# Moving the diagonal matrix of a gather step behind the dot product of the following step

## The chip, the cores and the metric

The kernel runs on one core of a Trainium2 chip. The time is that of one execution on the device, in microseconds (us). The core has a matmul engine (TensorE, PE in the profile; its weight loads are PEld), a vector engine (VectorE, DVE), an activation engine (ScalarE, ACT), a general engine (GpSimd, POOL) that here issues the gathers, and SyncE (SP), which issues the plain transfers. Each engine executes its own instructions in the order written and waits for the others by semaphores.

## The reference

One inference step of an encoder of two layers for 256 prompt tokens and 32 sample tokens, 1024 features each. Each layer is a mixer (a gated delta rule with a linear recurrence in layer 0, differential attention in layer 1) and behind it a channel mixer with 16,384 experts of a single neuron. The expert part is what this change touches:

```python
qry = (xb @ w_query).reshape(PEER_BLOCK, PEER_HEADS, 2, PEER_DQ // 2)
sc = jnp.einsum('thpd,pnd->thpn', qry, sub_keys)
s1, i1 = lax.top_k(sc[:, :, 0], PEER_TOPK)
s2, i2 = lax.top_k(sc[:, :, 1], PEER_TOPK)
...
top_s, sel = lax.top_k(cand_s, PEER_TOPK)
idx = jnp.take_along_axis(cand_i, sel, axis=-1)
gate = jax.nn.softmax(top_s, axis=-1)
act = jax.nn.gelu(jnp.einsum('thed,td->the', u_emb[idx], xb))
return jnp.einsum('the,thed->td', gate * act, v_emb[idx])
```

Each token has 8 heads of 16 chosen experts, 128 in all. For each chosen expert a row u and a row v of 1024 floats are gathered; the dot product of u with the token goes through a gelu, is multiplied by the gate, and weights v in the sum.

## The kernel before

Work on the experts is cut into 576 **gather steps**, numbered m from 0. A step handles 128 tokens with one expert each: a gather of 128 rows of 8 KB (u and v side by side, 1 MB) into one of the 8 slots of the ring `UV`, slot m % 8. Four engines take part, each in the order of m:

- POOL waits until the slot is free (`uv_free`) and issues the gather (L510). A list of 8 indices is copied ahead (L503).
- DVE waits for the landing, computes the 128 dot products (L1131), waits for the gelu of the same step, and builds the diagonal matrix DG = identity × gelu × gate (L1134). At each step with c = m % 16 = 0 it first copies the 16 gates of the next 16 steps (L1126), and at c = 15 it waits for its last diagonal.
- ACT applies the gelu to the dot products (L706).
- PE waits for the diagonal and multiplies it with the v half of the slot, as four matmul records into the accumulator in PSUM (L1510), and then frees the slot. The sum over the 128 experts of a token is thus formed in PSUM.

The steps form six units, which begin at m = 0, 32, 160, 288, 320 and 448: per layer 32 steps of sample tokens and twice 128 of prompt tokens. All units begin at c = 0 and end at c = 15. At the end of a unit PE closes the accumulator (L1523), and DVE adds it to the residual (L1149); PE begins the next unit only behind that.

Other work is put between the steps, by hand, at written step numbers: each engine calls `upto` to do its steps up to some m and then does its part of a mixer. `loop` does 16 steps an iteration. The order is: the first 32 steps between picks; a loop of 8 iterations over the steps 32 to 159, in which each iteration begins with a pick (the top-16 search of one head: L1072 to L1102) for later steps; then steps 160 to 447, with the mixer of layer 1 between them; and a last loop over the steps 448 to 575, with nothing between. The numbers for the middle part come from a table made by `step_plan`:

```python
for ps, m, misc, qkv, head, smp, out, q in ((0, 160) + PACE[0], (1, AHEAD) + PACE[1]):
    for kind, n, k in (("norm2", 1, misc), ("qkv", 24, qkv), ("head", 10, head), ("smp", 4 * (1 - ps), smp),
                       ("on", 1, misc), ("out", 8, out), ("norm3", 1, misc), ("q", 18 - 2 * ps, q)):
```

PE uses the same table but lags two steps behind it (PE_LAG = 2), except next to the edge of a unit: when PE reaches the mixer work of number m, it has done the steps up to m − 3.

Two **pick stages** matter below. In each, PE computes 16 query blocks (L1315) and their scores (L1553, L1555, or L1558), one pair of blocks for each pick of DVE; ScalarE copies blocks (L731) and scores (L723 to L726) out of PSUM in program order with its gelus. The first stage lies at the numbers 248, 251, 253, 256 and so on to 291, the second at 398, 400 and so on to 428. PE does a block, then the scores of the block before it. DVE does its steps up to the number of the odd block of a pair, then the pick of the pair before.

Of the kernel before, what the change touches and what calls it, by code (L numbers as in the profile page):

```python
# [29 lines left out]
UVS = 8  # L30
# [42 lines left out]
def build(nc, T):  # L73
# [4 lines left out]
    ALU, ACT, AX = mybir.AluOpType, mybir.ActivationFunctionType, mybir.AxisListType  # L78

    with ExitStack() as ctx:  # L80
        def sb(name, shape, dt=F):
            return ctx.enter_context(nc.sbuf_tensor("sb_" + name, shape, dt))
# [3 lines left out]
        def S(name):  # L86
            if name not in sems:
                sems[name] = ctx.enter_context(nc.semaphore(name))
            return sems[name]
# [41 lines left out]
        ident = sb("ident", [128, 128])  # L131
# [118 lines left out]
        gl = sb("gl", [128, 8])  # L250
        gst = sb("gst", [128, 16])
        DG = sb("DG", [128, UVS, 128])
# [32 lines left out]
        def at(i, value):  # L285

            return value if i is None else i * 16 + value

        class Steps:
# [6 lines left out]
            def edge(self, which):  # L296
                for q, (_, _, first, n) in enumerate(UNITS):
                    if which == "begin" and self.m == first:
                        self.begin(q)
                    if which == "end" and self.m == first + n:  # L300
                        self.end(q)
# [534 lines left out]
        def _(eng):  # L836
            v = nc.vector
# [111 lines left out]
            for bt, (u0, u1) in enumerate(BT):  # L949
# [14 lines left out]
                for u in range(u0, u1):  # L964
                    c = c0 + 128 * (u - u0)
# [139 lines left out]
            def gate_of(q):  # L1105
# [10 lines left out]
                ch.link(v.reciprocal(gsum[:, 0:nh], gsum[:, 0:nh]))  # L1116
                ch.link(v.tensor_tensor(gt, gt, top.to_broadcast([128, nh, 16]), ALU.mult))

            def step(m, i=None):

                q = max(k for k in range(6) if UNITS[k][2] <= m)
                c0, xt, m0, _ = UNITS[q]
                c, sl = m % 16, m % UVS
                if c == 0:
                    g0 = c0 + m - m0
                    v.tensor_copy(gst[:, :], gate[:, g0:g0 + 16] if i is None else gate[:, bass.ds(i * 16 + g0, 16)])\  # L1126
                        .then_inc(S("gates"), 1)
                    eng.wait_ge(S("gates"), m // 16 + 1 if i is None else i + (m // 16 + 1))
                landed = 16 * (m // UVS + 1)
                eng.wait_ge(S(f"uv_in{sl}"), landed if i is None else i * 32 + landed)  # L1130
                v.tensor_tensor_reduce(UV[:, sl, 0:D], UV[:, sl, 0:D], Hn[:, xt, :], 1.0, 0.0,  # L1131
                                       ALU.mult, ALU.add, dots[:, sl:sl + 1]).then_inc(S("dots"), 1)
                eng.wait_ge(S("gelu"), at(i, m + 1))
                v.tensor_scalar(DG[:, sl, :], ident[:, :], gl[:, sl:sl + 1], gst[:, c:c + 1],  # L1134
                                ALU.mult, ALU.mult).then_inc(S("diag"), 1)
                if c == 15:
                    eng.wait_ge(S("diag"), at(i, m + 1))

            def end(q):
# [7 lines left out]
                for half in range(2):  # L1147
                    o = X[:, xt, 512 * half:512 * half + 512]
                    r = v.tensor_tensor(o, o, PS[:, 6 + half, :], ALU.add)  # L1149
                    if half:  # L1150
                        r.then_inc(S("x_peer"), 1)

            run = Steps(eng, step, end=end)

            def picks(ps, upto):
# [603 lines left out]
```

## Time and profile before

| what | value |
| --- | --- |
| time, median of 3 runs | 2196.11 us |
| the runs | 2196.11, 2195.97, 2197.49 us |
| span of the profiled execution | 2197.3 us |
| mean granted clock of TensorE | 0.915 |
| busy: PE, DVE, POOL, ACT | 1761.6, 1405.6, 691.1, 379.4 us |
| moved from and to memory | 696.16 MB, 317 GB/s on average |
| gathered by POOL's queue | 604.02 MB, 68.9% of the 16 DMA engines' span |

The page gives busy time and idle time by groups of instructions. A row such as "x2304 | 1144.1, 641 | 301.1 <-DVE" reads: 2304 instructions, busy 1144.1 us in all, 641 ns each, and 301.1 us in which their engine was idle just before one of them, mostly until DVE released it. A timeline row has the start in us from the begin of the span, the duration, engine, line, operation, output and input, how many neighbouring instructions are merged (x), and in brackets the idle time ahead of it and what ended that. A row of PE with x4 is one gather step, x8 two, x12 three. A window's row has the stretch and its length, then the busy time (and count) of PE, PEld, DVE, ACT and POOL, TensorE's granted clock (1.00 is full speed), the DMA share and GB/s. A row of the chain of waits is start, duration, and the piece of work.

### The profile page before, as it was taken

What the parts mean: (1) busy time and instruction counts of PE and PEld (TensorE: products, weight loads), DVE (VectorE), ACT (ScalarE), POOL (GpSimd) and SP (SyncE); (2) the same over time, 40 slices, a digit from 0 to 9 for tenths busy, and PEclk for the clock granted to TensorE, in tenths of its full rate; (3) what the DMA queues carried; (4) which work ended last, traced back from release to release, by engine and by line L of the source; (5) the groups of instructions that cost most, each with busy time, mean ns of one, the idle gap of its engine ahead of it and who ended that gap; (6) DMA issues with size and microseconds to landing.
All of it is one profiled execution on the core that took longest, in us unless ns stands there. A gap on an engine that the chain in (4) does not pass through costs nothing.

```text
span 2197.3 us, 21194 instructions
## 1 busy us (share of the span) xinstructions
PE 1761.6 (80%) x6456; PEld 1001.9 (46%) x6456; DVE 1405.6 (64%) x3449; ACT 379.4 (17%) x1208; POOL 691.1 (31%) x738
## 2 busy tenths in 40 slices
PE   7978888777767778988698875998878877777776
PEld 6767875323223325754265542554445543322222
DVE  4464258877777774356446887554665896766665
ACT  2242022100000002142202111101421101111111
POOL 2032101334434451233223221333333324444441
PEclk9989999898878889999799987999889988999999
DMA  4310226889998999999688975999989978999997
GB/s 148 116 75 1 68 87 249 324 330 388 388 388 354 383 383 376 372 327 359 264 319 339 390 299 197 398 418 421 363 318 419 408 293 331 390 422 422 422 422 303
DMA packets 108846, 696.16 MB, mean 317 GB/s; under 512 B 12640, under 2 KB 12768, under 8 KB 34528
## 3 DMA queue, kind: packets, MB, share of 16 engines
q0 software_dynamic: 82944, 604.02, 68.9%
q1 hardware_dynamic: 24960, 89.98, 10.9%
q10 hardware_dynamic: 864, 1.16, 0.1%
q8 instruction: 44, 0.72, 0.1%
q14 instruction: 34, 0.28, 0.0%
HBM read 690.20 MB, written 4.90 MB: 316 GB/s over the span
## 4 chain that ended last, share of the span: by engine, by line
PE 45%; DVE 23%; DMA 19%; issue 7%; ACT 3%; POOL 1%; DVEq 0%; POOLq 0%; SPq 0%; ACTq 0%
PE PS L1510 21%; DMA sb_AR<-in_uv,sb_idst 19%; PE PS L1315 11%; DVE sb_AR L1131 5%; PE PS L1493 4%; DVE sb_DG L1134 2%; PE PS L1428 2%; PE PS L1591 2%; DVE sb_AR L1082 1%; DVE sb_AR L1075 1%; POOL sb_AR L510 1%; ACT sb_gl L706 1%; DVE sb_AR L1076 1%; DVE sb_AR L1079 1%; DVE sb_AR L1072 1%
## 5 line engine op out<-in xcount | busy, mean ns | idle before, releaser
L1510 PE MATMUL PS<-sb_AR,sb_DG 128*128 128x512 f32 x2304 | 1144.1, 641 | 301.1 <-DVE sb_DG L1134 285.3
L510 POOL DMA_INDIRECT sb_AR<-in_uv,sb_idst x576 | 610.8, 1060 | 1176.5 <-PE PS L1510 1118.0
L1510 PEld LDWEIGHTS PS<-sb_AR,sb_DG 128*128 128x128 f32 x2304 | 443.5, 204 | 916.7 <-DVE sb_DG L1134 463.2
L1131 DVE CUSTOM_DVE_ANT_0 sb_AR<-sb_AR,sb_Hn 128x1024 f32<-128x1024 f32 x576 | 704.6, 1223 | 160.3 <-DMA sb_AR<-in_uv,sb_idst 156.6
L1134 DVE TENSOR_SCALAR sb_DG<-sb_ident,sb_gl,sb_gst 128x128 f32<-128x128 f32 x576 | 222.7, 387 | 273.7 <-ACT sb_gl L706 273.7
L706 ACT ACTIVATE sb_gl<-sb_dots 128x1 f32<-128x1 f32 x576 | 116.7, 203 | 1228.3 <-DVE sb_dots L1131 1227.8
L1315 PE MATMUL PS<-sb_hT,sb_W 128*128 128x288 f32 (+2 forms) x1664 | 297.7, 335 | 0.8 <-ACT sb_hT L568 0.8
L1315 PEld LDWEIGHTS PS<-sb_hT,sb_W 128*128 128x128 f32 x1664 | 257.2, 192 | 64.3 <-issue 30.3
L1493 PEld LDWEIGHTS PS<-sb_W,sb_mixT 128*128 128x128 f32 x768 | 90.7, 196 | 9.8 <-issue 7.7
L1493 PE MATMUL PS<-sb_W,sb_mixT 128*128 128x128 f32 x768 | 90.9, 279 | 1.7 <-DVE sb_mixT L1045 1.7
L503 POOL COPY sb_idst<-sb_idx 128x8 uint32 (+1 forms) x72 | 24.4, 339 | 118.7 <-DVE sb_idx L1102 118.3
L1059 DVE TENSOR_TENSOR sb_X<-sb_X,PS 128x512 f32<-128x512 f32 x12 | 7.7, 684 | 77.4 <-PE PS L1493 77.4
L1072 DVE MAX8 sb_AR<-sb_AR 128x8 f32<-128x128 f32 (+1 forms) x108 | 32.8, 332 | 26.0 <-ACT sb_AR L726 20.1
L1591 PEld LDWEIGHTS PS<-sb_W,sb_hT 128*128 128x128 f32 x384 | 45.4, 192 | 7.7 <-issue 7.7
L1131 DVE DVE_READ_ACCUMULATOR2_ANT sb_dots<- 128x1 f32 x576 | 48.1, 83 | 0.0
L706 ACT ACT_TABLE_LOAD x36 | 46.2, 1283 | 3.0 <-DVE sb_dots L1131 1.8
L1302 PE MATMUL PS<-sb_ident,sb_Hn 128*128 128x128 f32 x96 | 20.7, 386 | 32.3 <-DVE sb_Hn L857 32.3
L1591 PE MATMUL PS<-sb_W,sb_hT 128*128 128x128 f32 x384 | 45.5, 275 | 0.0
L1079 DVE MAX8 sb_AR<-sb_AR 128x8 f32<-128x128 f32 (+1 forms) x108 | 32.9, 333 | 4.1
L1075 DVE FIND_INDEX8 sb_AR<-sb_AR 128x8 uint32<-128x128 f32 (+1 forms) x108 | 35.6, 329 | 0.0
L1082 DVE FIND_INDEX8 sb_AR<-sb_AR 128x8 uint32<-128x128 f32 (+1 forms) x108 | 34.7, 329 | 0.0
L1076 DVE MATCH_REPLACE8 sb_AR<-sb_AR 128x128 f32<-128x128 f32 (+1 forms) x108 | 34.6, 320 | 0.0
(315 smaller groups left out, 1101.6 us busy)
## 6 DMA issues: line engine op xcount, KB each, us to landing
sb_W<-in_w SPq DMA_DIRECT2D x144, 512.0 KB, 7.2
sb_AR<-in_uv,sb_idst POOLq DMA_INDIRECT x576, 11.3
sb_gB<-in_gains SPq DMA_DIRECT2D x7, 512.0 KB, 8.0
sb_AR<-in_kc SPq DMA_DIRECT2D x2, 1024.0 KB, 9.7
sb_AR<-in_vc SPq DMA_DIRECT2D x2, 1024.0 KB, 17.9
sb_X<-in_x SPq DMA_DIRECT2D x3, 512.0 KB, 5.2
out_o_v<-sb_AR SPq DMA_DIRECT2D x1, 1536.0 KB, 17.4
out_o_y<-sb_Hn SPq DMA_DIRECT2D x3, 512.0 KB, 7.4
```

The lines of the kernel that those rows point to most:

```text
L510: g.indirect_dma_start(UV[:, s, :], None, T[f"uv{l}"], bass.IndirectOffsetOnAxis(ap=idst[:, 8 * half + s:8 * half + s + 1], axis=0)).then_ ...
L706: s.activation(gl[:, o:o + 1], dots[:, o:o + 1], ACT.Gelu_apprx_tanh).then_inc(S("gelu"), 1)
L1075: ch.add(v.max_index(ind(i)[:, 0:8], val(i)[:, 0:8], src(i)))
L1076: ch.add(v.match_replace(tmp(i), val(i)[:, 0:8], src(i), -3.0e38))
L1079: ch.add(v.max(val(i)[:, 8:16], tmp(i)))
L1082: ch.add(v.max_index(ind(i)[:, 8:16], val(i)[:, 8:16], tmp(i)))
L1131: v.tensor_tensor_reduce(UV[:, sl, 0:D], UV[:, sl, 0:D], Hn[:, xt, :], 1.0, 0.0, ALU.mult, ALU.add, dots[:, sl:sl + 1]).then_inc(S("dots"), 1)
L1134: v.tensor_scalar(DG[:, sl, :], ident[:, :], gl[:, sl:sl + 1], gst[:, c:c + 1], ALU.mult, ALU.mult).then_inc(S("diag"), 1)
L1315: r = mm(PS[:, bank, 0:n], blkw(bb % WSLOTS, k), hT[:, k, c0:c0 + n], start=(k == 0), stop=(k == KT - 1))
L1493: r = mm(PS[:, 2 * t + j // 4, 128 * (j % 4):128 * (j % 4) + 128], mixT[:, k, 128 * t:128 * t + 128], blkw(bb % WSLOTS, k), start=(k == 0) ...
L1510: r = mm(PS[:, 6 + half, :], DG[:, sl, :], UV[:, sl, o:o + 512], start=False, stop=False, skip_group_check=True)
L1591: r = mm(PS[:, j % 4, 128 * i:128 * i + 128], hT[:, k, c:c + 128], blkw(bb % WSLOTS, k), start=(k == 0), stop=(k == KT - 1))
```

## The change

DVE's gather step no longer waits for its own gelu. The diagonal of step m − 1 is built behind the dot product of step m. Only at c = 15, the last of 16 steps, are two diagonals built, that of m − 1 and that of m, so that nothing is left over at the end of 16 steps. A step with c = 0 builds none. Whatever DVE does between two calls of `upto`, it does with the last diagonal still to come, unless the last step had c = 15. The other engines' programs are as they were.

```diff
+            def diagonal(m, i):
+
+                c, sl = m % 16, m % UVS
+                eng.wait_ge(S("gelu"), at(i, m + 1))
+                v.tensor_scalar(DG[:, sl, :], ident[:, :], gl[:, sl:sl + 1], gst[:, c:c + 1],
+                                ALU.mult, ALU.mult).then_inc(S("diag"), 1)
+
             def step(m, i=None):
...
                 v.tensor_tensor_reduce(UV[:, sl, 0:D], UV[:, sl, 0:D], Hn[:, xt, :], 1.0, 0.0,
                                        ALU.mult, ALU.add, dots[:, sl:sl + 1]).then_inc(S("dots"), 1)
-                eng.wait_ge(S("gelu"), at(i, m + 1))
-                v.tensor_scalar(DG[:, sl, :], ident[:, :], gl[:, sl:sl + 1], gst[:, c:c + 1],
-                                ALU.mult, ALU.mult).then_inc(S("diag"), 1)
+                if c:
+                    diagonal(m - 1, i)
                 if c == 15:
+                    diagonal(m, i)
                     eng.wait_ge(S("diag"), at(i, m + 1))
```

## Rows read from the trace of the kernel before

**Rows 1.** Page: chain by engine, two groups (busy, mean | idle before, releaser).

```profile
PE 45%; DVE 23%; DMA 19%; issue 7%; ACT 3%; POOL 1%; DVEq 0%; POOLq 0%; SPq 0%; ACTq 0%
...
L1510 PE MATMUL PS<-sb_AR,sb_DG 128*128 128x512 f32 x2304 | 1144.1, 641 | 301.1 <-DVE sb_DG L1134 285.3
...
L1134 DVE TENSOR_SCALAR sb_DG<-sb_ident,sb_gl,sb_gst 128x128 f32<-128x128 f32 x576 | 222.7, 387 | 273.7 <-ACT sb_gl L706 273.7
```

**Rows 2.** Windows: stretch, length, busy by engine, granted clock, DMA share, GB/s.

```profile
520.00:565.00 45.00, 30.86 (x64) 12.76 (x64) 34.26 (x87) 3.25 (x16) 16.23 (x18) 0.84 0.94 383
...
845.00:950.00 105.00, 104.53 (x609) 81.56 (x608) 36.24 (x75) 13.98 (x65) 23.17 (x27) 1.00 0.93 356
...
1210.00:1260.00 50.00, 43.98 (x178) 26.85 (x178) 44.79 (x140) 7.06 (x31) 14.36 (x16) 0.97 0.99 387
...
1700.00:1760.00 60.00, 52.09 (x233) 32.50 (x231) 52.28 (x171) 6.43 (x31) 18.89 (x21) 0.94 1.01 408
...
2000.00:2120.00 120.00, 95.58 (x193) 32.81 (x194) 76.90 (x148) 13.58 (x51) 49.17 (x55) 1.00 1.01 422
```

**Rows 3.** Timeline of the final loop's end, DVE and PE.

```profile
2179.86 1.23 DVE L1131 CUSTOM_DVE_ANT_0 sb_AR<-sb_AR,sb_Hn 128x1024 f32<-128x1024 f32 x1 [0.63 <-DMA sb_AR<-in_uv,sb_idst]
...
2182.32 1.23 DVE L1131 CUSTOM_DVE_ANT_0 sb_AR<-sb_AR,sb_Hn 128x1024 f32<-128x1024 f32 x1 [0.61 <-DMA sb_AR<-in_uv,sb_idst]
...
2183.82 0.34 DVE L1134 TENSOR_SCALAR sb_DG<-sb_ident,sb_gl,sb_gst 128x128 f32<-128x128 f32 x1 [0.27 <-ACT sb_gl L706]
...
2184.22 1.98 PE L1510 MATMUL PS<-sb_AR,sb_DG 128*128 128x512 f32 x4 [0.48 <-DVE sb_DG L1134]
```

**Rows 4.** Timeline behind a pick of the loop over steps 32 to 159.

```profile
523.70 1.23 DVE L1131 CUSTOM_DVE_ANT_0 sb_AR<-sb_AR,sb_Hn 128x1024 f32<-128x1024 f32 x1 [0.18 <-DVE sb_gst L1126]
...
525.21 0.35 DVE L1134 TENSOR_SCALAR sb_DG<-sb_ident,sb_gl,sb_gst 128x128 f32<-128x128 f32 x1 [0.27 <-ACT sb_gl L706]
...
525.47 1.22 DVE L1131 CUSTOM_DVE_ANT_0 sb_AR<-sb_AR,sb_Hn 128x1024 f32<-128x1024 f32 x1
...
525.61 5.59 PE L1510 MATMUL PS<-sb_AR,sb_DG 128*128 128x512 f32 x7 [11.23 <-DVE sb_DG L1134]
...
530.19 0.96 POOL L510 DMA_INDIRECT sb_AR<-in_uv,sb_idst  x1 [13.87 <-PE PS L1510]
```

**Rows 5.** The chain of waits between 2052 and 2058 us.

```profile
2047.85 15.18 DMA sb_AR<-in_uv,sb_idst
```

**Rows 6.** Timeline of the first pick stage, PE and DVE.

```profile
1216.39 3.70 PE L1510 MATMUL PS<-sb_AR,sb_DG 128*128 128x512 f32 x8
...
1223.47 1.22 DVE L1131 CUSTOM_DVE_ANT_0 sb_AR<-sb_AR,sb_Hn 128x1024 f32<-128x1024 f32 x1
...
1225.37 7.11 PE L1510 MATMUL PS<-sb_AR,sb_DG 128*128 128x512 f32 x12 [2.55 <-DVE sb_DG L1134]
...
1232.28 0.48 DVE L1072 MAX8 sb_AR<-sb_AR 128x8 f32<-128x128 f32 x2
...
1300.17 2.34 PE L1315 MATMUL PS<-sb_hT,sb_W 128*128 128x160 f32 x16
...
1300.99 1.22 DVE L1131 CUSTOM_DVE_ANT_0 sb_AR<-sb_AR,sb_Hn 128x1024 f32<-128x1024 f32 x1
...
1312.53 0.49 DVE L1072 MAX8 sb_AR<-sb_AR 128x8 f32<-128x128 f32 x2 [2.66 <-ACT sb_AR L724]
```

**Rows 7.** Timeline of one period of the second pick stage, DVE and PE.

```profile
1730.95 1.22 DVE L1131 CUSTOM_DVE_ANT_0 sb_AR<-sb_AR,sb_Hn 128x1024 f32<-128x1024 f32 x1
...
1732.85 6.56 PE L1510 MATMUL PS<-sb_AR,sb_DG 128*128 128x512 f32 x8 [4.17 <-DVE sb_DG L1134]
...
1737.99 0.48 DVE L1072 MAX8 sb_AR<-sb_AR 128x8 f32<-128x128 f32 x2
...
1746.31 1.22 DVE L1131 CUSTOM_DVE_ANT_0 sb_AR<-sb_AR,sb_Hn 128x1024 f32<-128x1024 f32 x1
```

**Rows 8.** Timeline of the sample attention, PE.

```profile
1025.86 8.49 PE L1510 MATMUL PS<-sb_AR,sb_DG 128*128 128x512 f32 x12 [2.92 <-DVE sb_DG L1134]
```

## The prediction

> **What bounds the kernel now.** I read the page first. The profiled execution spans 2197.3 us, 1.2 us (0.05%) above the median of 2196.11, so a sum made against the span can be carried to the median as it stands. No one engine bounds it: the chain that ended last is shared out over PE, DVE and the gather DMA. The group of the gather step's matmuls (L1510) is idle 301.1 us, nearly all of it put down to the diagonal L1134, and L1134 itself is idle 273.7 us behind the gelu [rows 1]. That last number, 0.47 us a step on average, is what the change goes at. The typical wait is 0.27 us, as the single steps show [rows 4].
>
> Next I read the windows, because what 0.27 us is worth differs by stage [rows 2]. In the final loop the DMA share is 1.01 at 422 GB/s and DVE is busy 76.9 of 120 us: DMA-bound. In the qkv stretch (845 to 950) PE is busy 104.53 of 105 us: PE-bound. In the two pick stages, where DVE picks experts between the steps (1210 to 1260, 1700 to 1760), DVE is busy about 90%: there the gelu wait is on the path, but so is everything that PE owes DVE. In the loop over steps 32 to 159 (520 to 565) the granted clock is 0.84, PE waits, and the DMA is not full.
>
> Then the timeline of one piece of each. In the final loop two dot products start 2.46 us apart, the second after 0.61 us of waiting for its gather [rows 3]. Whatever DVE does in the 0.27 us, the next landing sets the pace.
>
> **The change part by part.** It adds and removes no instruction: the tensor_scalar of step m is issued by DVE after the dot product of m+1, except at c = 15, where the diagonals of steps 14 and 15 stand together behind the dot of 15. So three things move. DVE no longer idles behind its own gelu: a step that DVE alone bounds falls from 1.77 us (525.47 − 523.70 [rows 4]) to about 1.50. PE gets each diagonal one dot later. And whatever DVE does between two steps (a pick of some 8 us, 15.36 − 7.04 in [rows 7], an attention wait, a norm) now stands ahead of the last diagonal that was due before it; PE, in program order, stands at that diagonal with all its mixer work behind it, and POOL's refill of the slot stands behind PE.
>
> *Final loop and other DMA-bound stretches.* PE's step, and with it the refill, come about one period (2.46 us) later. A gather of this loop takes 15.18 us from issue to landing on the chain [rows 5] although the DMA is full, so requests queue there for longer than 2.46 us, and a later issue shortens the queue, not the stream. Cost 0; without that cover it would be a bubble of up to 2.46 us once per loop, not per step. The qkv stretch is PE-bound: 0 too.
>
> *Loop 32 to 159.* Each of 8 iterations begins with a pick, across which PE idles 11.23 us and the DMA runs dry: POOL has been idle 13.87 us when the first refill goes out at 530.19, and it waits for PE's first step, which waits for the diagonal at 525.21 [rows 4]. That diagonal now stands behind the dot that began at 525.47. Without the gelu wait and the diagonal ahead of it that dot begins at about 524.95, takes 1.22, so the diagonal begins at about 526.2, 1.0 later. The iteration is bounded by first refill to last landing, so it gets 1.0 longer: 8 × 1.0 = 8.0 (bounds 0, if the DMA makes it up, and 8 × 1.2). Two more first steps behind such a gap (steps 16 and 448): 2.0.
>
> *First pick stage* (steps 250 to 287, five steps to a pick). Call E the start of the first dot behind a pick (1223.47). Before, the next pick starts at 1232.28 = E + 8.8, five steps of 1.76 [rows 6]. PE used the pick: at 1216.39, while DVE picked, it did two steps (3.70), the query block that the next pick needs, and its scores, and then idled 2.55 us. After, the second of these two steps is held until E + 1.25, so PE starts it at E + 1.65, ends it at E + 3.5 (1.85, half of 3.70), the block (2.34) at E + 5.8, the scores, two pairs of small matmuls that I put at 0.7, at about E + 6.5. ScalarE works in order, block and score copies ahead of the gelu of the third step, so this gelu comes at about E + 7, its diagonal at E + 7.2, then one more dot and diagonal: pick at about E + 8.9. Warm that is +0.1, for five times 0.27 saved pay for it. But PE then has idled some 7 us, and idle of that kind has shown a fall of the clock: behind 2.55 us of idle the twelve matmuls took 7.11, behind 4.17 us eight took 6.56 where the eight at 1216.39 took 3.70 [rows 6, 7]. A slow step costs 3.28 − 1.85 = 1.4 and the block behind it may be slow as well. I take +1.5 for three picks (bounds 0.1 and 3.0) and 2.7 for the one that follows two picks in a row. The last pick, that of the sample, already waits for PE: it starts at 1312.53 after 2.66 us of idle. Its chain starts with the block at 1300.17 and would now start at 1300.99 + 1.65 + 1.85 = 1304.5, 4.3 later [rows 6]; with a slow start (+1.8) I take 6.1. Sum 4.5 + 2.7 + 6.1 = 13.3. The pick whose held step is 255 has c = 15, is flushed, and costs nothing.
>
> *Second pick stage* (steps 398 to 428, four steps to a pick). The period is 1746.31 − 1730.95 = 15.36 [rows 7]. After, by the same steps with a shorter block, the next pick could start at about E + 6.5 warm instead of E + 7.0, where it started at 1737.99 (−0.6); the held step now follows a PE idle of over 4 us, and eight matmuls behind such a gap lost 6.56 − 3.70 = 2.9. So +2.3 a period, for five of the seven picks that wait on the step before (held steps 403, 407, 411, 419, 423; 399 and 415 are flushed): 11.5 (bounds −3 and 15). Step 427 is held over two picks, its slot is refilled late: 2.2 (bounds 0 and one step of the stream, 2.46).
>
> *What bears on the price of a slow start.* The Trainium skill, in "TensorE: Matmul & The Clock Gate", section "HAM oscillation — how this bites in real kernels", says that where PE works in short bursts with idle between, its clock falls anew for each burst and each pays the slow start. The rows agree so far (the granted clock is 0.84 in a stretch with such gaps, 1.00 where there are none [rows 2]). By that rule all held periods pay 2.9 instead of the 1.5 and 2.3 taken, and the sum would be about 7 us higher.
>
> *Unit ends.* Every unit ends on c = 15, so PE's last two steps become ready together. At the end PE began its last step at 2184.22, 0.40 behind the diagonal of 2183.82 [rows 3]; after, two steps of 1.85 start 0.25 earlier: +1.6, say 1.5, at five of six ends: 7.5 (bounds 0 and 9). The end at step 320 lies in a DMA-bound stretch.
>
> *Mixer work of layer 1 between the steps.* In the sample attention PE waits 2.92 us for a diagonal behind the softmax and then does the steps that are owed ahead of its transposes [rows 8]. One more step is owed after: 1.5, and the second time, where a cache load follows, 2.6. Similar held steps at the output adds and third norms: 5.0, at two head copies: 2.2. These places are estimated from the same 1.4 to 1.9 for a held step (bounds 0 and twice that). The second norms, which DVE reaches sooner, give back 1.7.
>
> Sum: 8.0 + 2.0 + 13.3 + 11.5 + 2.2 + 7.5 + 4.1 + 5.0 + 2.2 − 1.7 = 54.1. On the median: 2196.1 + 54.1 = 2250 us, slower by 2.5%.
>
> **Rivals.** *Faster: the waits go and nothing takes their place.* About 68 steps (40 in the first pick stage, 28 in the second) run at DVE's pace; 68 × 0.27 = 18.4 us: 2178. For it: DVE busy at 90% there [rows 2], 273.7 us of waits on gelu [rows 1]. Against: PE's block for the next pick would have to be done during a pick, and its step is held. It decides by whether that block matters: if the scores are ready before E + 8.5 even so, the gain stands.
>
> *Warm: the order of waits as I say, but PE's clock doesn't fall further.* Then the first pick stage costs 0.3 + 4.3, the second −3.0, the rest as above: 54.1 − (13.3 − 4.6) − (11.5 + 3.0) = 31: 2227. For it: in the first pick stage's window the clock is 0.97 [rows 2].
>
> *Hidden: no change.* Where DMA-bound stretches follow each loss, a fuller queue gives it back: 2196. Against: in the pick stretches' ends and the loop the DMA is not full.
>
> *Worse: the ring is one slot short behind every pick,* a bubble of 2.46 us in each of some 11 pick periods beside the sum: 27 more, 2277. For it: POOL idles 13.87 us there [rows 4].
>
> **How the numbers follow.** Forecast as summed 0.52 (2235 to 2265), warm 0.22 (2213 to 2235), worse 0.12 (2265 to 2290), faster 0.09, hidden 0.05. The range, 2212 to 2272, leaves out the last two and half of the worse case, just under 2 in 10. A difference of 0.2% (4.4 us) is about what a measurement of this kernel can tell from none. Faster 0.09, same 0.05, slower 0.86.
>
> **What would show it.** L1134's idle behind gelu should fall from 273.7 to little, with waits of 1 to 4 us left in the pick stretches, and L1510's idle behind L1134 should grow. PE should idle some 7 us across a pick of the first stage and start behind E + 1.65; pick periods of the second should be about 17.7 us, but stay near 15 where c = 15 flushed the step. Iterations of the loop should be 1.0 longer, the final loop's 2.46 us period unchanged. If the pick periods got shorter, the faster rival was right; if the loop iterations did not grow, the DMA made it up.

## The result and the profile after

The changed kernel takes 2222.03 us (median of four runs, 2219.93 to 2225.82), against 2196.8 us before: slower by 1.16%, ratio 1.0116 with a 95% interval of 1.0100 to 1.0132. Forecast were 2250 us and "slower". The sign is right, the time lies in the range, but the loss is 25 us instead of 54: less than half. The profiled execution spans 2218.2 us, 20.9 more than that of before; a second profile of the changed kernel, taken later, spans 2223.1 us, 25.8 more.

The page of the changed kernel, the chain by engine and the groups that answer to [rows 1], with the dot product beside them (L1510, L1134 and L1131 of before are now L1517, L1123 and L1138). The last row is the dot product on the page of before:

```profile
PE 48%; DVE 21%; DMA 21%; issue 6%; ACT 2%; POOL 1%; DVEq 0%; POOLq 0%; SPq 0%; ACTq 0%
...
L1517 PE MATMUL PS<-sb_AR,sb_DG 128*128 128x512 f32 x2304 | 1141.7, 636 | 339.9 <-DVE sb_DG L1123 332.3
...
L1138 DVE CUSTOM_DVE_ANT_0 sb_AR<-sb_AR,sb_Hn 128x1024 f32<-128x1024 f32 x576 | 702.2, 1223 | 319.1 <-DMA sb_AR<-in_uv,sb_idst 315.6
...
L1123 DVE TENSOR_SCALAR sb_DG<-sb_ident,sb_gl,sb_gst 128x128 f32<-128x128 f32 x576 | 200.8, 349 | 114.6 <-ACT sb_gl L706 114.3
...
L1131 DVE CUSTOM_DVE_ANT_0 sb_AR<-sb_AR,sb_Hn 128x1024 f32<-128x1024 f32 x576 | 704.6, 1223 | 160.3 <-DMA sb_AR<-in_uv,sb_idst 156.6
```

The aim was met: the diagonal's idle time behind the gelu fell from 273.7 to 114.3 us. It did not become time gained. The dot product now waits 315.6 us for gathers instead of 156.6, so the 159 us saved behind the gelu came back there, and PE waits 332.3 us for diagonals, 47 more than before. What is left of the gelu wait is 50 waits, 2.3 us each on average. On the chain PE's share rose from 45 to 48%, DVE's fell from 23 to 21%.

The end of the final loop, DVE and PE, answering to [rows 3]:

```profile
2199.36 1.23 DVE L1138 CUSTOM_DVE_ANT_0 sb_AR<-sb_AR,sb_Hn 128x1024 f32<-128x1024 f32 x1 [0.99 <-DMA sb_AR<-in_uv,sb_idst]
...
2201.82 1.23 DVE L1138 CUSTOM_DVE_ANT_0 sb_AR<-sb_AR,sb_Hn 128x1024 f32<-128x1024 f32 x1 [0.97 <-DMA sb_AR<-in_uv,sb_idst]
...
2202.97 0.70 DVE L1123 TENSOR_SCALAR sb_DG<-sb_ident,sb_gl,sb_gst 128x128 f32<-128x128 f32 x2
...
2203.37 3.70 PE L1517 MATMUL PS<-sb_AR,sb_DG 128*128 128x512 f32 x8 [0.48 <-DVE sb_DG L1123]
...
2206.91 1.88 PE L1530 MATMUL PS<-sb_ZR 128*128 128x512 f32 x4
```

The dots are 2.46 us apart as before, and the idle time ahead of one has grown from 0.61 to 0.97: DVE is ready earlier and waits for the same landing. At 2203.37 PE does the last two steps in one go (x8), 3.70 us, where it had one step to do before.

Behind a pick of the loop, answering to [rows 4]:

```profile
524.92 1.23 DVE L1138 CUSTOM_DVE_ANT_0 sb_AR<-sb_AR,sb_Hn 128x1024 f32<-128x1024 f32 x1 [0.18 <-DVE sb_gst L1133]
...
526.07 1.22 DVE L1138 CUSTOM_DVE_ANT_0 sb_AR<-sb_AR,sb_Hn 128x1024 f32<-128x1024 f32 x1
...
527.22 0.34 DVE L1123 TENSOR_SCALAR sb_DG<-sb_ident,sb_gl,sb_gst 128x128 f32<-128x128 f32 x1
...
527.62 4.64 PE L1517 MATMUL PS<-sb_AR,sb_DG 128*128 128x512 f32 x5 [10.72 <-DVE sb_DG L1123]
```

The dots of the iteration's first two steps now stand back to back, 1.15 us apart instead of 1.77, but the first diagonal comes behind the second dot: PE starts 2.70 us behind the first dot, where it had started 1.91 behind it. (The last row shows five records because the view ends there.)

The windows, answering to [rows 2]. The second and third are pick periods (from the first dot behind a pick to the first dot behind the next) that begin with a held step, one whose diagonal is still owed from before the pick, one of each stage; the fourth is the next such period of the second stage:

```profile
520.00:565.00 45.00, 32.17 (x64) 12.67 (x64) 31.43 (x82) 3.24 (x16) 19.21 (x18) 0.85 0.91 368
1231.31:1250.18 18.87, 16.40 (x60) 9.54 (x60) 15.05 (x48) 2.61 (x11) 4.07 (x6) 0.91 0.98 370
1745.94:1762.16 16.22, 12.81 (x52) 8.08 (x52) 13.57 (x45) 1.59 (x8) 4.23 (x5) 0.89 0.88 318
1762.16:1777.31 15.15, 13.61 (x65) 8.83 (x66) 14.09 (x48) 1.59 (x8) 5.22 (x4) 1.00 0.96 373
2000.00:2120.00 120.00, 95.13 (x195) 33.09 (x194) 73.35 (x148) 13.59 (x51) 49.74 (x55) 1.00 1.01 422
```

And two periods of the second pick stage in the timeline, answering to [rows 7]: in the first the held step is slow, in the second it is not.

```profile
1742.19 1.88 PE L1517 MATMUL PS<-sb_AR,sb_DG 128*128 128x512 f32 x4
...
1745.94 1.22 DVE L1138 CUSTOM_DVE_ANT_0 sb_AR<-sb_AR,sb_Hn 128x1024 f32<-128x1024 f32 x1
...
1747.48 2.79 PE L1517 MATMUL PS<-sb_AR,sb_DG 128*128 128x512 f32 x4 [3.41 <-DVE sb_DG L1123]
...
1750.07 2.84 PE L1322 MATMUL PS<-sb_hT,sb_W 128*128 128x128 f32 x16
...
1753.57 0.35 DVE L1123 TENSOR_SCALAR sb_DG<-sb_ident,sb_gl,sb_gst 128x128 f32<-128x128 f32 x1 [2.20 <-ACT sb_gl L706]
...
1753.83 0.48 DVE L1072 MAX8 sb_AR<-sb_AR 128x8 f32<-128x128 f32 x2
...
1762.16 1.22 DVE L1138 CUSTOM_DVE_ANT_0 sb_AR<-sb_AR,sb_Hn 128x1024 f32<-128x1024 f32 x1
...
1763.70 1.98 PE L1517 MATMUL PS<-sb_AR,sb_DG 128*128 128x512 f32 x4 [3.41 <-DVE sb_DG L1123]
...
1765.52 1.95 PE L1322 MATMUL PS<-sb_hT,sb_W 128*128 128x128 f32 x16
...
1768.77 0.49 DVE L1072 MAX8 sb_AR<-sb_AR 128x8 f32<-128x128 f32 x2
```

PE does one step at 1742.19 during the pick and then has nothing until the diagonal that DVE builds behind the first dot after the pick, 3.41 us. In the first period the held step takes 2.79 us and the block behind it 2.84; the third step's diagonal waits 2.20 us for its gelu, and the pick begins at E + 7.89 (1753.83 − 1745.94). In the second they take 1.98 and 1.95, and the pick begins at E + 6.61 (1768.77 − 1762.16). The order of waits is the one predicted, and E + 6.5 was the forecast without a slow start. The two slow pieces take 0.81 and 0.89 us longer than the fast ones, 1.70 together.

Where the time went is read from the starts of the dot products of chosen steps. The table has the length of each part in us, from the dot of one step to that of the next, worked out from the timelines of the profiled executions; the column "again" is the change in the second profile of the changed kernel:

| steps | before | after | change | again | priced in the prediction |
| --- | --- | --- | --- | --- | --- |
| start to 32 | 479.4 | 479.4 | 0.0 | +2.2 | +2.5 (first step, one end) |
| 32 to 159, the loop | 341.5 | 349.9 | +8.4 | +8.1 | +8.0 |
| 159 to 246, layer 1's mixer, first half | 349.0 | 355.2 | +6.3 | +8.4 | +8.4 with the end at 160 |
| 246 to 288, first pick stage | 171.9 | 172.8 | +0.9 | +1.1 | +14.8 with the end at 288 |
| 288 to 398, mixer, second half | 348.5 | 349.6 | +1.1 | +1.2 | +2.7 |
| 398 to 440, second pick stage | 149.9 | 150.0 | +0.1 | +0.4 | +13.7 |
| 440 to 575 | 342.2 | 344.9 | +2.7 | +3.0 | +2.5 |
| behind the last dot | 15.0 | 16.4 | +1.4 | +1.4 | +1.5 |

The parts "priced" sort the prediction's terms by place; what it had in one number for both halves of the mixer (5.0, 2.2, −1.7) is shared equally. Of the 33 us between the forecast and the first profile, 27 lie in the two pick stages; of the 28 to the second, again 27. The other parts are right to within about 3 us each.

### The profile page after: what moved, and what is told of

Its sections match the earlier page's. It is cut to its first block, busy times and chain, and to the rows that moved or that the text cites. A ratio compares the mean times of both kernels' runs of the same rounds, so it can differ in the third digit from the quotient of the medians.

```text
span 2218.2 us, 21194 instructions
## 1 busy us (share of the span) xinstructions
PE 1757.1 (79%) x6456; PEld 994.5 (45%) x6456; DVE 1359.2 (61%) x3449; ACT 378.4 (17%) x1208; POOL 686.0 (31%) x738
## 3 DMA queue, kind: packets, MB, share of 16 engines
q10 hardware_dynamic: 864, 1.16, 0.1%
## 4 chain that ended last, share of the span: by engine, by line
PE 48%; DVE 21%; DMA 21%; issue 6%; ACT 2%; POOL 1%; DVEq 0%; POOLq 0%; SPq 0%; ACTq 0%
PE PS L1517 24%; DMA sb_AR<-in_uv,sb_idst 21%; PE PS L1322 11%; PE PS L1500 4%; DVE sb_AR L1138 4%; PE PS L1435 2%; DVE sb_AR L1082 2%; DVE sb_DG L1123 1%; PE PS L1598 1%; DVE sb_AR L1075 1%; DVE sb_AR L1076 1%; DVE sb_AR L1079 1%; DVE sb_AR L1072 1%; DVE sb_AR L1097 1%; DVE sb_AR L1100 1%
## 5 line engine op out<-in xcount | busy, mean ns | idle before, releaser
L1517 PE MATMUL PS<-sb_AR,sb_DG 128*128 128x512 f32 x2304 | 1141.7, 636 | 339.9 <-DVE sb_DG L1123 332.3
L1138 DVE CUSTOM_DVE_ANT_0 sb_AR<-sb_AR,sb_Hn 128x1024 f32<-128x1024 f32 x576 | 702.2, 1223 | 319.1 <-DMA sb_AR<-in_uv,sb_idst 315.6
L1517 PEld LDWEIGHTS PS<-sb_AR,sb_DG 128*128 128x128 f32 x2304 | 433.6, 201 | 956.4 <-DVE sb_DG L1123 534.3
L1123 DVE TENSOR_SCALAR sb_DG<-sb_ident,sb_gl,sb_gst 128x128 f32<-128x128 f32 x576 | 200.8, 349 | 114.6 <-ACT sb_gl L706 114.3
L1138 DVE DVE_READ_ACCUMULATOR2_ANT sb_dots<- 128x1 f32 x576 | 47.8, 83 | 0.0
L731 ACT ACTIVATE sb_AR<-PS 128x288 f32<-128x288 f32 (+2 forms) x48 | 15.9, 331 | 179.2 <-PE PS L1322 179.2
```

What stands on the lines that cost most here:

```text
L1517: r = mm(PS[:, 6 + half, :], DG[:, sl, :], UV[:, sl, o:o + 512], start=False, stop=False, skip_group_check=True)
```

## The experiments

All runs were timed in five rounds beside the kernel before on the same chip; "against before" is the ratio with its 95% interval. They ran on three chips, on which the kernel before took 2198.3, 2199.6 and 2200.6 us (it took 2196.8 beside the changed kernel above), so a difference between two kernels that weren't timed side by side is uncertain by some 4 us.

The steps that hold their diagonal back are chosen by one function, `held`. In place of the change's two ifs the later kernels have

```python
flush()                      # builds a diagonal that is still owed
if held(m):
    pending.append((m, i))
else:
    diagonal(m, i)
```

so that `held = (m % 16 != 15)` is the change itself.

**One part of the change alone: the pick stages, and the loop.**

```diff
-                return m % 16 != 15
+                return m % 16 != 15 and (246 <= m < 288 or 396 <= m < 428)
```

> The later diagonal only in the two pick stages (steps 246 to 287 and 396 to 427), every other step as before. The prediction's sum priced these stages at +27 us (13.3 + 11.5 + 2.2). Theory read from the trace of after: a held period costs under 1 us and flushed periods give back 1.7, so the stages come out at -4 to +1 us against before. The rival in which the waits simply go: -18 us.

```diff
-                return m % 16 != 15
+                return m % 16 != 15 and 32 <= m < 160
```

> The later diagonal only in the steps 32 to 159, every other step as before. Theory: each of 8 iterations gets 1.0 us longer because the first refill behind the pick goes out 1.0 later, and the end of the unit adds 1.5, so +9 to +10 us against before. Rival (the DMA makes the late refill up and the loss sits in the middle part): 0 to +2.

The picks alone: 2208.08 us, ratio 1.0038 (1.0023 to 1.0053), so 5 to 12 us slower. None of the three expectations held: not the prediction's 27, and not the near-zero read from the trace of after. In its profile the first stage costs +5.3 us (177.2 against 171.9) and the second +2.3; the latter is no more than the +2.6 that the same stage shows in the profile of the loop alone, which changes nothing there. In the changed kernel the first stage costs only +0.9. Of the 4.4 us between the two, 2.5 arise before step 256: in the changed kernel the third norm ahead of the stage makes step 246 late, by +2.9 on the way from step 244, and most of this lateness seems to be absorbed at the start of the stage, for from step 246 to 251 the changed kernel gains 4.8 us on before, this one 2.2. The rest lies mostly in two periods with a slower start (+2.9 and +2.4 instead of +1.7 and +1.9).

The loop alone: 2210.74 us, ratio 1.0053 (1.0036 to 1.0071). In the profile the loop is 8.2 us longer and the end of its unit 1.1, as expected.

**The first step of 16 builds its own diagonal.**

```diff
-                return m % 16 != 15
+                return m % 16 not in (0, 15)
```

> The change, but the first step of each 16 builds its own diagonal at once, as before. Theory: PE's first step behind a pick of the loop and behind other gaps is no longer late, so the loop loses its +8 and two or three more first steps 1.0 each: 9 to 11 us less than the changed kernel, +14 against before. Rival (the loop's loss is the doubled last step, not the first): no difference from the changed kernel, +24.

2215.99 us, ratio 1.0080 (1.0064 to 1.0096): 17.7 us slower than before, where the changed kernel was 25.2 slower, so 7.5 less instead of 9 to 11. The loop takes 342.9 us in the profile against 349.9 with the change and 341.5 before, and PE starts 1.91 us behind the first dot again. So 7.0 of its 8.4 us come from the late first step. The other 1.4 are not traced; they are as much as the loop varies in the profiles that change nothing in it (340.1 to 341.5).

**A diagonal that is owed is built before DVE turns to other work.**

```diff
                 def upto(kind, j=0):
                     run.upto(PLAN[ps, kind, j])
+                    if kind in ('norm2', 'head', 'smp', 'on', 'out', 'norm3'):
+                        flush()
...
                 def tile1(h):
+                    flush()
                     eng.wait_ge(S("sc"), 16 * ps + 2 * h + 2)
```

(with the same `flush()` ahead of `tile0`, `sample` and the gates' softmax)

> The change, but a diagonal that is still owed is built before DVE goes on to other work (a pick, a norm, attention, the output adds); inside runs of steps it stays late. Theory: the held steps of the sample attention, norms, outputs and picks go, and the 0.27 us a step saved in the pick stages stays: 15 to 25 us less than the changed kernel, 0 to +8 against before, with the loop's +8 and the doubled ends still in it. Rival (the loss is in the loop and the ends alone and holding costs nothing): within 4 us of the changed kernel.

2188.95 us, ratio 0.9966 (0.9955 to 0.9977): 9 us faster than before, where at best no change was expected, and 33 us below the changed kernel. The first pick stage takes 163.3 us (before 171.9), the second 142.9 (149.9), the first half of the mixer 347.1 (349.0) and the second 341.7 (348.5). The loop keeps its loss (349.8).

**The price of the slow start.** PE is given zeros to multiply while it would wait for a held step; they add nothing to the sum.

```diff
                 def upto(kind, j=0):
-                    run.upto(lagging(PLAN[ps, kind, j]))
+                    end = lagging(PLAN[ps, kind, j])
+                    if kind == "q" and j >= 4 and j % 2 == 0 and (end - 1) % 16 != 15 and end - 1 > run.m:
+                        run.upto(end - 1)
+                        for k in range(6):
+                            mm(PS[:, 6 + k % 2, :], ZR[:, 0:128], ZR[:, :], start=False, stop=False,
+                               skip_group_check=True)
+                    run.upto(end)
```

> The changed kernel, and in the pick stages PE does six matmuls with zeros (about 2.6 us, they add nothing to the sum) while it would idle some 3.5 us ahead of the held step. Theory: a held period costs because that step and the block behind it run at the lower clock; with PE kept busy the step takes 1.9 to 2.0 instead of 2.8 to 3.6 us, the next pick of the second stage starts at about E + 6.6 instead of E + 7.9, and some nine periods save 1 us each: 6 to 10 us less than the changed kernel. Rival (the price is the order of work alone): within 3 us of the changed kernel.

> The changed kernel itself, on the same chip as its neighbours: +23 to +27 us against before by every theory.

2231.23 us, ratio 1.0142 (1.0121 to 1.0163), against 2221.95 us, 1.0106 (1.0085 to 1.0126), for the changed kernel beside it: 9 us worse. The filling was mis-sized, as its timeline shows:

```profile
1769.48 5.31 PE L1586 MATMUL PS<-sb_ZR 128*128 128x512 f32 x12
...
1772.65 0.34 DVE L1123 TENSOR_SCALAR sb_DG<-sb_ident,sb_gl,sb_gst 128x128 f32<-128x128 f32 x1
...
1774.63 1.88 PE L1517 MATMUL PS<-sb_AR,sb_DG 128*128 128x512 f32 x4
...
1776.34 1.95 PE L1322 MATMUL PS<-sb_hT,sb_W 128*128 128x128 f32 x16
```

The six matmuls are twelve records, 5.31 us. The held step can begin only at 1774.63, some 1.6 us behind the end of its diagonal (1772.65 + 0.34). It and the block behind it were fast, but late. Half as many (`range(3)`):

> The changed kernel with half as much filling ahead of a held step: in the trace the six matmuls of the run before took 5.2 us, not 2.6 (each is two records), and held the step up themselves. Three should take 2.6 us and end before the held diagonal is there. Clock theory: held step 1.9 to 2.0 us, its block 1.95 or 2.34, the next pick of the second stage at E + 6.6 to 6.8, held periods of the second stage no longer than before (15.4 us or less); 6 to 10 us less than the changed kernel. Rival (the order of work alone): the pick stays at E + 7.5 or later, total within 3 us of the changed kernel.

2214.27 us, ratio 1.0063 (1.0044 to 1.0083): 13.7 us above the kernel before beside it, where the changed kernel was 22.3 above in its second timing. That is 8 to 9 us less, as the clock theory had it. A period of the second stage, then its window and that of the period of the first stage shown above:

```profile
1733.25 2.74 PE L1586 MATMUL PS<-sb_ZR 128*128 128x512 f32 x6
...
1735.28 1.22 DVE L1138 CUSTOM_DVE_ANT_0 sb_AR<-sb_AR,sb_Hn 128x1024 f32<-128x1024 f32 x1
...
1736.82 1.98 PE L1517 MATMUL PS<-sb_AR,sb_DG 128*128 128x512 f32 x4 [0.83 <-DVE sb_DG L1123]
...
1738.64 1.95 PE L1322 MATMUL PS<-sb_hT,sb_W 128*128 128x128 f32 x16
...
1741.52 0.48 DVE L1072 MAX8 sb_AR<-sb_AR 128x8 f32<-128x128 f32 x2
```

```profile
1735.28:1749.84 14.56, 13.73 (x59) 8.12 (x58) 13.57 (x46) 1.59 (x8) 4.83 (x4) 1.00 1.02 417
1236.38:1253.55 17.17, 16.28 (x65) 9.69 (x64) 15.04 (x49) 2.62 (x11) 5.06 (x6) 1.00 1.01 406
```

PE's clock stays at 1.00, the held step takes 1.98 us, and the pick begins at E + 6.24 and the period is 14.56, where the changed kernel's slow one took 16.22 (1762.16 − 1745.94) and that of before 15.36 [rows 7]. A slow start thus costs 1.7 us in this stage, and without it a held period is 0.8 shorter than before. In the first stage the corresponding period is 17.17 instead of 18.87: again 1.7. The profile has four slow starts fewer than the changed kernel's, each worth 1.7. It doesn't show the whole gain of 8 to 9 us: its execution was the slowest of the five (it spans 2218.9 us), the two stages together are 4.7 us shorter than in the first profile of the changed kernel, and the first stage alone only 0.3, since two of its other periods are 1.0 and 0.5 longer. Filling doesn't help everywhere either: step 419, 2.53 us behind the end of its filling, took 3.63 us at a granted clock of 0.53.

**The last step but one builds its own diagonal.**

```diff
-                return m % 16 != 15
+                return m % 16 not in (14, 15)
```

> The change, but the step with c = 14 builds its own diagonal at once, so that PE's last two steps of a unit are not ready together. Theory: the ends of units lose their +1.2 to +1.5 at five places: 5 to 8 us less than the changed kernel. Rival (the end is set by something else): within 2 us of it.

2221.28 us, ratio 1.0103 (1.0084 to 1.0123), no different from the changed kernel beside it. Expected were 5 to 8 us less. In the profile the part behind the last dot is 15.6 us, between 15.0 before and 16.4 with the change, and the ends at 32, 160 and 448 give back 0.8 each. The doubled pair had only moved one step up: PE now does steps 13 and 14 together, and with 1.85 us of work in a period of 2.46 it catches up 0.6 us a step.

**The versions that use what was found.** All three repairs together, then the change in the pick stages alone with nothing held across a pick, then everywhere but in the loops and in the last four steps of a unit, with owed diagonals built ahead of other work.

```diff
-                return m % 16 != 15
+                return m % 16 not in (0, 14, 15)
```

> All three repairs: the steps with c = 0 and c = 14 build their own diagonal, and a diagonal that is owed is built ahead of other work. Theory: the gelu waits saved in the pick stages stay (about 68 steps less those exempted, some 14 us), the loop's +8 and the ends' +6 go: 18 to 24 us below before, about 2176. Rival (the repairs overlap or the DMA takes it back): no better than the version with the owed diagonals alone, 9 us below before.

```diff
-                return m % 16 != 15
+                return m % 16 != 15 and (246 <= m < 288 or 396 <= m < 428)
...
                 def tile1(h):
+                    flush()
```

> The later diagonal only in the two pick stages, and there built before a pick begins. Theory: nothing is held across a pick, each of about 68 steps less one per period saves 0.27 us: 13 to 20 us below before. Rival (the stages are bounded by something else than DVE's own steps): 0 to -5.

```diff
-                return m % 16 != 15
+                return m % 16 not in (0, 15) and not 32 <= m < 160 and m < 448 and not any(0 < u[2] + u[3] - m <= 4 for u in UNITS)
```

> The later diagonal only outside the two loops (steps 32 to 159 and 448 to 575), not at c = 0 or c = 15, not in the last four steps of a unit, and built before DVE goes on to other work. Theory: the loops and ends are as before, the middle part saves as in the combined version: 20 to 25 us below before, some 2 to 4 better than the combined version. Rival: no better than the combined version (-20).

| version | median | against before |
| --- | --- | --- |
| three repairs | 2178.71 us | 0.9908 (0.9889 to 0.9927) |
| pick stages, nothing held | 2180.50 us | 0.9915 (0.9897 to 0.9933) |
| middle part, nothing held | 2176.21 us | 0.9895 (0.9873 to 0.9917) |

All are about 1% faster than before; their intervals overlap, so none is shown to be the best. The second does only what the first rival of the prediction supposed, and gains 20 us, which that rival forecast as 18.4; in its profile the two stages are 9.4 and 8.9 us shorter than before. A pick between two dots of its first stage, and with the last row the end of the same period before:

```profile
1219.15 1.22 DVE L1148 CUSTOM_DVE_ANT_0 sb_AR<-sb_AR,sb_Hn 128x1024 f32<-128x1024 f32 x1
...
1226.26 0.48 DVE L1072 MAX8 sb_AR<-sb_AR 128x8 f32<-128x128 f32 x2
...
1234.59 1.22 DVE L1148 CUSTOM_DVE_ANT_0 sb_AR<-sb_AR,sb_Hn 128x1024 f32<-128x1024 f32 x1
...
1240.60 1.22 DVE L1131 CUSTOM_DVE_ANT_0 sb_AR<-sb_AR,sb_Hn 128x1024 f32<-128x1024 f32 x1
```

The whole period is 15.4 us, where it was 17.13 before (1240.60 − 1223.47, the latter in [rows 6]). Inside it a step takes 1.40 us instead of 1.76; the prediction had 1.50.

## Why the prediction was half right

*The sign and its mechanism: right.* PE in program order stands at a diagonal that DVE builds only behind its next dot product, and what is behind it waits. Removing the held diagonals alone turns +25 us into −9 us.

*The loop: right.* +8.4 measured for 8.0, and the cause of 7.0 of it shown by the run in which the first step of 16 builds its own. PE's start behind the pick moved by 0.8 us where the prediction had 1.0.

*Final loop and DMA-bound stretches: right.* The final loop's period is unchanged; DVE's idle time in it grew instead.

*Unit ends: right within 1.5 us.* 1.4 at the last, 1.1 to 1.4 at 32, 160, 288 and 448, for 1.5 each. The end at 320, priced at nothing, cost 1.1 in the profile, but the next 27 steps gave it back.

*The pick stages: wrong, and this is the step that failed.* The sum had "+1.5 for three picks", "2.7 for the one that follows two picks in a row", "So +2.3 a period, for five of the seven picks", and put at nothing the periods whose step isn't held (255, 399 and 415, "flushed"). The table sets this against the first profile. A period is named by the step whose dot begins it. The second profile agrees to within 0.4 us, and in the profile of the loop alone, which changes nothing here, the periods from 256 to 285 and from 404 to 427 are as before to within 0.1 us (398 and 428 are 0.7 and 1.9 longer there, so these two say less).

| part | priced | measured |
| --- | --- | --- |
| 246 to 256, ahead of the first period | 0 | −4.7 |
| 256, 398 and 416: no held step | 0 | −2.1, −2.6, −1.7 |
| 261, 266, 271 | 1.5 each | +1.7, 0.0, −0.9 |
| 276, behind two picks | 2.7 | +1.9 |
| 404, 408, 412, 420, 424 | 2.3 each | +0.9, +0.9, −0.6, +1.1, +0.9 |
| 281, the sample's pick | 6.1 | +4.2 |
| 286 with the end at 288; 428 with the late refill | 1.5; 2.2 | +0.8; +1.3 |

The nine periods of lines three to five begin with a held step; they cost 5.9 us instead of 18.7. The parts priced at nothing gave back 11.1. Three things were wrong.

First, the price of the slow start. For the second stage the prediction took 2.9 us from eight slow matmuls of before; 1.7 was measured, in both stages, as the difference between a period with PE kept busy and one without. In the first stage its +1.5 fits the one of the three that was slow. It had PE idle "some 7 us across a pick"; ahead of a held step of that stage the trace has 2.5 to 3.6, and 10.45 behind two picks, since PE still does an odd block, its scores and one step while DVE picks. Without a slow start the sum's own working was good: E + 6.5 against the 6.61 measured (6.24 with the gap filled), and for the last pick of the first stage, which starts behind 6.86 us of idle, +4.2 against 4.3. The 1.8 added to that one for the clock did not appear.

```profile
1311.60 1.21 DVE L1138 CUSTOM_DVE_ANT_0 sb_AR<-sb_AR,sb_Hn 128x1024 f32<-128x1024 f32 x1
...
1313.13 1.99 PE L1517 MATMUL PS<-sb_AR,sb_DG 128*128 128x512 f32 x4 [2.46 <-DVE sb_DG L1123]
...
1314.95 2.34 PE L1322 MATMUL PS<-sb_hT,sb_W 128*128 128x160 f32 x16
...
1327.30 0.49 DVE L1072 MAX8 sb_AR<-sb_AR 128x8 f32<-128x128 f32 x2 [6.86 <-ACT sb_AR L724]
```

Second, not every held period was slow: of the ten (with the sample's), those of 266, 271, 281 and 412 began with a held step of 2.0 us. In the profile of after the period that begins with the dot of step 408 was slow (clock 0.89 in the window above), that of step 412 was not (1.00), each behind the same 3.41 us of idle.

Third, no credit was given to the steps that hold nothing. Each period without a held step gained 1.7 to 2.6 us (steps 416 to 420: 13.68 instead of 15.39), as the first rival has it. The 4.7 us at the start of the first stage are such a gain in part: 2.3 in the run of the pick stages alone, where the norm ahead isn't late.

The Trainium skill, in "TensorE: Matmul & The Clock Gate", section "HAM oscillation — how this bites in real kernels", describes a kernel in which every burst of matmuls behind a wait for data starts slow. The trace agrees in kind: six of the ten held periods began slow, and the filled gaps show that the clock is the price. That every held period pays, which the prediction weighed as 7 us more, the trace does not bear out.

*The rivals.* The total came out near the "warm" rival (2227), but by luck and not by its mechanism: slow starts did occur, and cost some 8 us in all by the filled gaps, while the gains that it left out made up for them. The "faster" rival failed at the place it named: the block for the next pick stood behind the held step. With that step built ahead of the pick, its sum is right to 2 us. "Hidden" is excluded by the measured interval, and "worse" by the periods: none but the sample's grew by more than 1.9 us. The 13.87 us of POOL's idle time that spoke for it are from the loop [rows 4], not from these stages.

*Left open.* Why equal idle times are followed by a slow step in one period and not in the next. It is not chance from run to run alone: in the second profile of the changed kernel the same two steps took 2.76 and 1.98 us, behind 3.41 and 3.40 us of idle. In the run of the pick stages alone four held steps behind 3.4 us took 3.41, 3.25, 2.43 and 1.98. And why the pick stages' cost differs by 4 us between the kernel with the change everywhere and that with it there alone: that the late third norm is absorbed at the start of the stage is read from the starts of steps 246 and 251, not tested.

## What to carry to other kernels

Delaying a hand-over by one step is safe only inside a run of equal steps, and even there the first step of the run comes late; before the engine turns to anything longer, hand over what is owed. Here that one rule turned 1.2% slower into 0.3% faster, and with those steps left out where it only costs (first steps, loops, ends of units), 1% faster. When a stall is moved, list the work that stands behind the delayed instruction on each consumer, and give the steps that escape it their credit: a sum of losses alone is as wrong as a sum of gains. And a price for a slow clock is better taken from the idle gap that is most like the new one than from the worst one in the trace: the shorter gap in [rows 6] gives 7.11 − 3 × 1.85 = 1.6 us, near the 1.7 measured.

## What was not expected of the hardware

Three matmuls of 128x512 in full floats are six records of 0.46 us each (2.74 us for x6), and that much work in a 3.4 us gap of PE kept its granted clock at 1.00 through the whole period shown, where the empty gap gave 0.89 in one period and 1.00 in the next. And the spread from run to run is wide beside the differences looked for: the kernel with the change in the pick stages alone ran from 2197.10 to 2211.18 us in eleven runs.
